# Differential attention on one core: the two maps of a head combined while they are turned, with one value product per head

## The chip, the cores and the metric

The kernel runs on one core of a Trainium2 chip. It is written by hand, engine by engine: TensorE (PE in the profile) multiplies, VectorE (DVE) and ScalarE (ACT) do the elementwise work, GpSimd (POOL) does next to nothing, SyncE (SP) issues the weight loads. The engines run side by side and wait for each other through semaphores. The metric is the device time of one execution in microseconds; several executions are taken, and their median counts.

## What is computed

The program is a whole forward pass: two layers of one model (attention, RWKV, two feed-forward stages) and two layers of a second one behind it. The change touches one stage, the differential attention of the second model, for 256 tokens, 8 heads, and two maps of width 64 in each head:

```python
q = q.reshape(bsz, seq, h, 2, d)          # h = 8 heads, 2 maps, d = 64
k = k.reshape(bsz, seq, h, 2, d)
v = v.reshape(bsz, seq, h, 2 * d)
lam_full = jnp.exp(jnp.sum(lamf[0] * lamf[1])) - jnp.exp(jnp.sum(lamf[2] * lamf[3])) + lambda_init
...
s = jnp.einsum('bqhcd,bkhcd->bhcqk', q_blk, k).astype(jnp.float32)
p = jax.nn.softmax(jnp.where(allowed, s, -jnp.inf), axis=-1)
p_diff = p[:, :, 0] - lam_full * p[:, :, 1]
return jnp.einsum('bhqk,bkhe->bqhe', p_diff.astype(v.dtype), v)
```

A query of chunk c (64 tokens) may look at the keys of chunks 0 to c. The output of each head is then normalised by its root mean square and goes through an output projection.

## The kernel before

All operands are f32. Tokens lie on the 128 partitions in two row tiles t = 0, 1. By the mask, row tile 0 needs 128 keys and row tile 1 needs 256, so a map has three 128 x 128 tiles (t, kt) = (0,0), (1,0), (1,1), and 384 score columns.

`attention()` (L948) is shared by all attentions of the program. The differential one calls it from `differential()` (L2087) with 16 maps, `diff=True` and `halves=True`. The work of a map m is a pipeline over the engines:

- TensorE, scores (L986): queries times keys, into a PSUM bank. With `halves`, the two maps of a head are issued together, on the two halves of the array's rows (64 each).
- VectorE, maxima (L1023): one pass that adds the mask, scales, writes the scores to SBUF and takes the row maximum, for each row tile.
- ScalarE, exps (L1072): exp with the maximum as bias, and the row sums, for each row tile.
- TensorE, turns (L997): three transposes of the exps, into another PSUM bank.
- ScalarE, copy (L1063): the turned tiles to SBUF.
- TensorE, products (L1005): turned tiles times values, three matmuls.
- VectorE, outputs: reciprocal of the row sums (L1035); for the second map of a head also the product with minus lambda (L1037, `nlam`); then the product of each row tile is scaled and written (L1046, first map), or scaled and added to the first map's output (L1044, second map). Row statistics of the finished head follow (L967).

The order on each engine is written out by a loop over i. Turns lag the scores by `TURN` = 2 maps and products by `MIX` = 3 maps. In iteration i TensorE issues the scores of maps i and i+1 (for even i), the turns of map i-2 and the products of map i-3. VectorE does the maxima of map i, then the outputs of map i-3; ScalarE copies the turned map i-2, then does the exps of map i. There are four buffers for exps, two banks for turned tiles, two for products, four for scores.

Behind the loop TensorE runs ten filler matmuls (L149) while VectorE forms the scales of all heads from the row statistics (L2110 to L2119) and ScalarE takes a root (L2102). The output projection begins with transposes of the scaled outputs (L437). The first norms of the program (L378) multiply by a diagonal of row scales instead of a plain identity; the 16 matmuls of one such norm are a like form to what the change adds.

## Time and profile before

| | us |
|---|---|
| median of 3 runs | 1690.74 |
| lowest and highest | 1688.20 and 1690.88 |
| the profiled execution | 1687.52 |
| span of its trace | 1685.70 |
| TensorE busy, whole span | 1647.3 (98%) |
| VectorE busy | 896.1 (53%) |
| ScalarE busy | 697.8 (41%) |
| GpSimd busy | 5.0 |
| first scores to last row statistics of this attention | 887.29 to 915.86 |

Times inside the trace count from the start of its span. A row of the timeline gives the start, the duration and the operation; rows that follow each other on an engine are merged ("x6"), and a note in brackets says how long the engine was idle before and what released it. Matmuls overlap: the start of the next one, not the duration of a row, tells what one costs. A plain f32 matmul leaves two rows, since it is made of two passes; a transpose leaves one. PEld is the loading of weights, which runs beside PE.

### The profile page before, as it was taken

How to read it: one execution, taken by the hardware profiler on the slowest of the kernel's cores; microseconds unless marked ns; L12 is line 12 of the kernel's file. 1: busy time of each engine (PE TensorE's matmuls, PEld its weight loads, DVE VectorE, ACT ScalarE, POOL GpSimd, SP SyncE). 2: the span in 40 equal slices, each digit the busy share in tenths (PEclk: the TensorE clock that was granted, in tenths of full speed). 3: DMA queues.
4: the chain of work that ended last, by engine and by line, in shares of the span. 5: the costliest groups of instructions: out<-in, count | busy, mean ns of one | idle time of the engine just before them, and what ended most of it. 6: DMA issues, size and time to landing. Idle time of an engine off the chain costs nothing.

```text
span 1685.7 us, 30187 instructions
## 1 busy us (share of the span) xinstructions
PE 1647.3 (98%) x12844; PEld 1288.1 (76%) x12844; DVE 896.1 (53%) x1932; ACT 697.8 (41%) x1347; POOL 5.0 (0%) x6
## 2 busy tenths in 40 slices
PE   9999999999999999999999999999989999999996
PEld 8889999787698699999887987555546798655553
DVE  6676565644567465658659765212126876521213
ACT  5576444433343354446548553111123655311111
POOL 0000000000000000000000000000000000000000
PEclk9999999999999999999999999999999999999998
DMA  8613453424200554535551446999992344699995
GB/s 343 250 76 151 160 216 131 165 100 150 89 3 13 228 186 160 216 107 194 199 186 40 176 167 261 425 424 426 423 421 76 113 186 172 261 426 424 425 425 226
DMA packets 36154, 371.69 MB, mean 220 GB/s; under 512 B 7200, under 2 KB 8352, under 8 KB 11184
## 3 DMA queue, kind: packets, MB, share of 16 engines
q1 hardware_dynamic: 32928, 364.09, 54.4%
q10 hardware_dynamic: 3088, 5.61, 1.0%
q8 instruction: 105, 1.72, 0.4%
q14 instruction: 33, 0.27, 0.0%
HBM read 368.63 MB, written 1.05 MB: 219 GB/s over the span
## 4 chain that ended last, share of the span: by engine, by line
PE 91%; DVE 5%; ACT 2%; DMA 1%; issue 1%; DVEq 0%; ACTq 0%
PE ps L660 41%; PE ps L2369 13%; PE ps L2392 6%; PE ps L884 3%; PE ps L2381 2%; PE ps L1005 2%; PE ps L1541 2%; PE ps L2352 2%; PE ps L1785 2%; PE ps L1754 2%; PE ps L986 1%; DMA ring<-in_w_moe 1%; PE ps L437 1%; PE ps L2856 1%; PE ps L2423 1%; PE ps L1768 1%
## 5 line engine op out<-in xcount | busy, mean ns | idle before, releaser
L660 PE MATMUL ps<-ffn_x_h,ffn_w 128*128 128x256 f32 x1408 | 257.4, 283 | 0.2
L2369 PE MATMUL ps<-ring,expert_inputs 128*64 128x256 f32 x1984 | 227.8, 382 | 0.7 <-DMA ring<-in_w_moe 0.7
L660 PEld LDWEIGHTS ps<-ffn_x_h,ffn_w 128*128 128x128 f32 x1408 | 221.2, 192 | 1.5 <-DVE ffn_x_l L499 0.5
L652 ACT CAST w_h<-ring 128x512 fp32r<-128x512 f32 x240 | 149.3, 624 | 138.1 <-PE ps L660 130.1
L660 PE MATMUL ps<-ffn_x_l,ffn_w 128*128 128x256 f32 x704 | 199.2, 283 | 0.0
L655 DVE TENSOR_TENSOR w_l<-ring,w_h 128x512 fp32r<-128x512 f32 x240 | 164.0, 689 | 66.0 <-ACT w_h L652 62.0
L2369 PEld LDWEIGHTS ps<-ring,expert_inputs 128*64 128x64 f32 x1984 | 137.0, 137 | 67.8 <-DMA ring<-in_w_moe 1.0
L655 DVE TENSOR_TENSOR ffn_w<-ring,ffn_w 128x1024 fp32r<-128x1024 f32 x132 | 155.8, 1220 | 20.9 <-ACT ffn_w L652 20.9
L660 PE MATMUL ps<-w_h,x_h 128*128 128x512 f32 x384 | 150.1, 391 | 0.0
L660 PE MATMUL ps<-w_h,x_l 128*128 128x512 f32 x384 | 149.5, 389 | 0.0
L660 PE MATMUL ps<-w_l,x_h 128*128 128x512 f32 x384 | 149.4, 389 | 0.0
L652 ACT CAST ffn_w<-ring 128x1024 fp32r<-128x1024 f32 x132 | 131.6, 1045 | 23.0 <-PE ps L660 23.0
L2504 ACT ACTIVATE routing<-ps 64x256 f32<-64x256 f32 x64 | 24.1, 377 | 272.3 <-PE ps L2369 272.3
L660 PEld LDWEIGHTS ps<-ffn_x_l,ffn_w 128*128 128x128 f32 x704 | 135.0, 192 | 0.7
L2631 DVE TENSOR_TENSOR routing<-routing,ps 64x256 f32<-64x256 f32 x64 | 27.2, 424 | 193.4 <-ACT routing L2504 193.4
L2392 PE MATMUL ps<-ring,routing 128*64 128x512 f32 x512 | 122.3, 598 | 0.8 <-DVE routing L2639 0.8
L660 PE MATMUL ps<-ffn_w,ffn_hid_h 128*128 128x512 f32 x352 | 108.8, 390 | 0.0
L1339 DVE SCALAR_TENSOR_TENSOR arena<-ps,cols,arena 128x255 f32<-128x255 f32 (+1 forms) x88 | 38.4, 478 | 89.8 <-ACT arena L1301 89.0
L660 PEld LDWEIGHTS ps<-w_h,x_l 128*128 128x128 f32 x384 | 72.1, 188 | 15.1
L660 PEld LDWEIGHTS ps<-w_h,x_h 128*128 128x128 f32 x384 | 72.1, 188 | 14.7
L660 PEld LDWEIGHTS ps<-w_l,x_h 128*128 128x128 f32 x384 | 72.1, 188 | 14.6
L2639 DVE COPY routing<-ps 128x128 f32<-128x128 f32 x64 | 18.5, 289 | 120.4 <-PE ps L2423 120.4
(377 smaller groups left out, 2657.4 us busy)
## 6 DMA issues: line engine op xcount, KB each, us to landing
ring<-in_w_moe SPq DMA_DIRECT2D x62, 2048.0 KB, 14.2
ring<-in_w_proj SPq DMA_DIRECT2D x37, 2048.0 KB, 7.8
ring<-in_w_ffn SPq DMA_DIRECT2D x22, 3072.0 KB, 10.2
ring<-in_w_moe SPq DMA_DIRECT2D x64, 1024.0 KB, 14.7
ring<-in_w_b_in SPq DMA_DIRECT2D x1, 2496.0 KB, 12.6
ring<-in_w_lora SPq DMA_DIRECT2D x1, 2048.0 KB, 7.6
rows<-in_w_moe SPq DMA_DIRECT2D x2, 1024.0 KB, 10.0
h<-in_w_moe SPq DMA_DIRECT2D x2, 1024.0 KB, 4.8
```

The source lines that it names most:

```text
L652: act.copy(high, x).then_inc(ready.up(), 1)
L655: return dve.tensor_tensor(low, x, high.bitcast(F32), ALU.subtract)
L660: last = pe.matmul(out, a[x], b[y], start=start and n == 0, stop=stop and n == 2, skip_group_check=True)
L884: last = pe.matmul(bank((n + 3 + m // 2) % 4)[:, (m % 2) * SEQ:(m % 2 + 1) * SEQ], w[:, k, m * P:(m + 1) * P], src[:, k, :], start=(k == 0 ...
L1005: last = pe.matmul(bank(o_bank[m % 2])[:, t * dv:(t + 1) * dv], pT[:, m % 2, c, :], v(m, kt), start=(kt == 0), stop=(kt == width[t] // P - 1))
L1339: ins = dve.scalar_tensor_tensor(x, gt[:, f, 0:SEQ - lag], col("conv_w", (layer * 3 + w) * FT + ft), x, ALU.mult, ALU.add)
L1541: last = pe.matmul(bank((n + 3 + t) % 4), mixes[x][:, k, t * P:(t + 1) * P], unit(i)[:, k, :], start=(k == 0), stop=(k == KD - 1))
L1754: last = pe.matmul(nt_out(q)[half(g), m % GROUP, w, :], x[1 - w], x[w], start=True, stop=True)
L1785: return pe.matmul(bank(OUT_BANK + 2 * t + u), xT[:, k, t * P:(t + 1) * P], w[:, k, :], start=(k == 0), stop=(k == KD - 1))
L2352: last = pe.matmul(o, parts_h[x][:, t, k * P:(k + 1) * P], put[:, t * D + q * QUAD:t * D + (q + 1) * QUAD], start=(t == 0 and x == 0), sto ...
L2369: last = pe.matmul(bank(0)[g * SLOTS_E:(g + 1) * SLOTS_E, 0:2 * P], x[:, k, e * SLOTS_E:(e + 1) * SLOTS_E], wg[g][:, k, :], start=(k == 0) ...
L2392: last = pe.matmul(bank(2)[c * SLOTS_E:(c + 1) * SLOTS_E, :], hids[:, f, :], wd[:, f, c * 512:(c + 1) * 512], start=(n % 2 == 0 and f == 0 ...
```

## The change

The differential attention gets a function of its own, `paired_attention()`, and its special cases leave `attention()`. It works in heads instead of maps.

The output of a head is r0 (P0 V) - lambda r1 (P1 V), where P0 and P1 are the exps of its maps, and r0, r1 the reciprocals of their row sums s0, s1. It is now formed as r0 ((P0 + c P1) V) with c = -lambda r1 s0, one number per query:

- VectorE forms the reciprocals of both maps at once (four numbers a row) and c (two numbers a row: the ratio).
- GpSimd multiplies the identity by c, for both row tiles, into a 128 x 256 buffer: two diagonal matrices.
- TensorE turns and combines at once: for each of the three tiles a plain matmul of the first map's exps with the identity, and one of the second map's exps with the diagonal, added in the same PSUM bank. (Before: one transpose for each tile of each map.)
- ScalarE copies once per head, and there is one set of products and one scaling per head, by r0.

The lags stay `TURN` = 2 and `MIX` = 3, but now count heads. Exps have room for three heads. The order per iteration i on VectorE is maxima of head i, ratio of head i-1, statistics of head i-4, outputs of head i-3; on ScalarE: exps of the first map, copy of head i-2, exps of the second map. GpSimd waits for the ratio and, from the third head on, for TensorE to have used the diagonal of two heads before.

The core of the diff (the new function, without its buffer declarations):

```diff
+        def paired_attention(q, k, v, o, scale, work):
...
+            DEPTH, TURN, MIX = 3, 2, 3
...
+            s_bank, p_bank, o_bank = ((6, 7), (0, 1)), (2, 3), (4, 5)
...
+                @block.tensor
+                def _(pe):
+                    for i in range(DIFF_HEADS + MIX):
...
+                        if i < DIFF_HEADS:
+                            if i >= 2:
+                                pe.wait_ge(s_out.sem, s_out.at(2 * T * (i - 1)))
+                            for t in range(T):
+                                for m in range(2):
+                                    last = pe.matmul(bank(s_bank[i % 2][m])[:, at[t]:at[t] + widths[t]], q(2 * i + m, t), k(2 * i + m)[:, 0:widths[t]], start=True, stop=True)
+                            last.then_inc(s_mm.up(), 1)
+                        if TURN <= i < DIFF_HEADS + TURN:
+                            hd = i - TURN
...
+                            if hd >= 2:
+                                pe.wait_ge(pT_ready.sem, pT_ready.at(hd - 1))
+                            pe.wait_ge(p_ready.sem, p_ready.at(2 * T * (hd + 1)))
+                            pe.wait_ge(diag_ready.sem, diag_ready.at(hd + 1))
+                            for c, (t, kt) in enumerate(tiles):
+                                pe.matmul(bank(p_bank[hd % 2])[:, c * P:(c + 1) * P], scores(hd, 0)[:, c * P:(c + 1) * P], ident[:], start=True, stop=False)
+                                last = pe.matmul(bank(p_bank[hd % 2])[:, c * P:(c + 1) * P], scores(hd, 1)[:, c * P:(c + 1) * P], diag[:, hd % 2, t, :], start=False, stop=True)
+                            last.then_inc(p_mm.up(), 1)
+                        if i >= MIX:
+                            hd = i - MIX
+                            pe.wait_ge(pT_ready.sem, pT_ready.at(hd + 1))
+                            if hd >= 2:
+                                pe.wait_ge(o_out.sem, o_out.at(hd - 1))
+                            for c, (t, kt) in enumerate(tiles):
+                                last = pe.matmul(bank(o_bank[hd % 2])[:, t * P:(t + 1) * P], pT[:, hd % 2, c, :], v(hd, kt), start=(kt == 0), stop=(kt == t))
+                            last.then_inc(o_mm.up(), 1)
+
+                @block.gpsimd
+                def _(pool):
+                    for hd in range(DIFF_HEADS):
+                        pool.wait_ge(ratio_ready.sem, ratio_ready.at(hd + 1))
+                        if hd >= 2:
+                            pool.wait_ge(p_mm.sem, p_mm.at(hd - 1))
+                        one = ident[:].rearrange("p (o s) -> p o s", o=1).broadcast_to([P, T, P])
+                        c = ratio[:, hd % 2, :].rearrange("p (t o) -> p t o", o=1).broadcast_to([P, T, P])
+                        pool.tensor_tensor(diag[:, hd % 2], one, c, ALU.mult).then_inc(diag_ready.up(), 1)
...
+                    def ratios(hd):
+                        b = hd % DEPTH
+                        dve.wait_ge(p_ready.sem, p_ready.at(2 * T * (hd + 1)))
+                        if hd >= DEPTH:
+                            dve.wait_ge(o_out.sem, o_out.at(hd - DEPTH + 1))
+                        link(dve, "dve_step", dve.reciprocal(rs[:, b], sums[:, b]))
+                        if hd >= 2:
+                            dve.wait_ge(diag_ready.sem, diag_ready.at(hd - 1))
+                        dve.scalar_tensor_tensor(ratio[:, hd % 2, :], rs[:, b, 1, :], nlam[:], sums[:, b, 0, :], ALU.mult, ALU.mult).then_inc(ratio_ready.up(), 1)
...
+                    for i in range(DIFF_HEADS + MIX):
+                        if i < DIFF_HEADS:
+                            maxima(i)
+                        if 1 <= i <= DIFF_HEADS:
+                            ratios(i - 1)
+                        if i > MIX:
+                            statistics(i - MIX - 1)
+                        if i >= MIX:
+                            outputs(i - MIX)
+                    statistics(DIFF_HEADS - 1)
...
+                    for i in range(DIFF_HEADS + TURN):
+                        if i < DIFF_HEADS:
+                            exps(i, 0)
+                        if i >= TURN:
+                            turned(i - TURN)
+                        if i < DIFF_HEADS:
+                            exps(i, 1)
```

How the order changes is seen at one head in the middle. TensorE before, from one set of scores on (`arena2_12` holds queries, keys, exps and turned tiles, `arena1_9` the values and outputs, `ident` the identity; `probs_ready` counts exps, `act_evacuated` copies of turned tiles):

```order
L986 MATMUL ps<-arena2_12 128x128 [waits scores_copied]
L986 MATMUL ps<-arena2_12 128x128
L986 MATMUL ps<-arena2_12 128x256 x2
L997 MATMUL ps<-ident,arena2_12 128x128 [waits act_evacuated,probs_ready]
L997 MATMUL ps<-ident,arena2_12 128x128 x2
L1005 MATMUL ps<-arena1_9,arena2_12 128x128 [waits dve_evacuated,act_evacuated]
L1005 MATMUL ps<-arena1_9,arena2_12 128x128 x2
L997 MATMUL ps<-ident,arena2_12 128x128 [waits act_evacuated,probs_ready]
L997 MATMUL ps<-ident,arena2_12 128x128 x2
L1005 MATMUL ps<-arena1_9,arena2_12 128x128 [waits dve_evacuated,act_evacuated]
L1005 MATMUL ps<-arena1_9,arena2_12 128x128 x2
```

and after, from one set of scores on (`conv_ready` is the semaphore of GpSimd's diagonals):

```order
L981 MATMUL ps<-arena2_12 128x128 [waits scores_copied]
L981 MATMUL ps<-arena2_12 128x128
L981 MATMUL ps<-arena2_12 128x256 x2
L992 MATMUL ps<-ident,arena2_12 128x128 [waits conv_ready,probs_ready,act_evacuated]
L993 MATMUL ps<-arena2_12 128x128
L992 MATMUL ps<-ident,arena2_12 128x128
L993 MATMUL ps<-arena2_12 128x128
L992 MATMUL ps<-ident,arena2_12 128x128
L993 MATMUL ps<-arena2_12 128x128
L1001 MATMUL ps<-arena1_9,arena2_12 128x128 [waits act_evacuated]
L1001 MATMUL ps<-arena1_9,arena2_12 128x128 x2
```

Two groups of three transposes and two groups of three products, each group with its waits, have become one group of six matmuls, which also waits for the diagonal, and one of three.

VectorE before, from the outputs of a first map to those of the second (`ISA` rows are the maxima and the reading of their result):

```order
L1035 RECIPROCAL stat<-stat 128x2 [waits probs_ready]
L1046 TENSOR_SCALAR arena1_9<-ps,stat 128x128 [waits product_ready,dve_step]
L1046 TENSOR_SCALAR arena1_9<-ps,stat 128x128
L967 BN_STATS arena0_0<-arena1_9 128x6 [waits dve_evacuated]
L1023 ISA arena2_12,stat<-ps,mask 128x128 [waits transposed,scores_ready]
L1023 ISA stat 128x1
L1023 ISA arena2_12,stat<-ps,mask 128x256
L1023 ISA stat 128x1
L1035 RECIPROCAL stat<-stat 128x2 [waits probs_ready]
L1037 TENSOR_SCALAR stat<-stat,nlam 128x2 [waits dve_step]
L1044 SCALAR_TENSOR_TENSOR arena1_9<-ps,stat,arena1_9 128x128 [waits dve_evacuated,product_ready,dve_step]
L1044 SCALAR_TENSOR_TENSOR arena1_9<-ps,stat,arena1_9 128x128
```

and after, from the maxima of a head's second map into the next head:

```order
L1026 ISA arena2_12,stat<-ps,mask 128x128
L1026 ISA stat 128x1
L1026 ISA arena2_12,stat<-ps,mask 128x256
L1026 ISA stat 128x1
L1034 RECIPROCAL stat<-stat 128x4 [waits dve_evacuated,probs_ready]
L1037 SCALAR_TENSOR_TENSOR stat<-stat,nlam 128x2 [waits conv_ready,dve_step]
L1048 BN_STATS arena0_0<-arena1_9 128x6 [waits dve_evacuated]
L1048 BN_STATS arena0_0<-arena1_9 128x6
L1042 TENSOR_SCALAR arena1_9<-ps,stat 128x128 [waits product_ready]
L1042 TENSOR_SCALAR arena1_9<-ps,stat 128x128
L1026 ISA arena2_12,stat<-ps,mask 128x128 [waits transposed,scores_ready]
L1026 ISA stat 128x1
```

The two outputs of the second map are gone, the reciprocals are one instruction of four numbers, the ratio takes the place of the product with lambda, and it stands right behind the maxima, before the outputs. Nothing else in the program moves on TensorE, VectorE or ScalarE; GpSimd's eight instructions stand ahead of the two it had.

## Rows read from the trace of the kernel before

**Rows 1.** Busy time: start:end, length, busy us (count) of PE, PEld, DVE, ACT, POOL, clock.

```profile
887.29:914.24 26.95, 24.97 (x210) 20.88 (x210) 24.02 (x131) 24.06 (x83) 0.00 (x0) 1.00 0.01 2
```

**Rows 2.** TensorE in order of time, one head: start us, us, engine, line, operation.

```profile
904.00 0.93 PE L986 MATMUL ps<-arena 64*128 64x128 f32 x8
904.86 0.55 PE L997 MATMUL ps<-ident,arena 128*128 128x128 f32 x3
905.24 0.83 PE L1005 MATMUL ps<-arena,arena 128*128 128x128 f32 x6
905.91 0.49 PE L997 MATMUL ps<-ident,arena 128*128 128x128 f32 x3
...
907.00 0.93 PE L986 MATMUL ps<-arena 64*128 64x128 f32 x8
```

**Rows 3.** VectorE in order of time, the same head.

```profile
904.28 0.27 DVE L1023 CUSTOM_DVE_ANT_0 arena<-ps,mask 128x128 f32<-128x128 f32 x1
...
904.83 0.16 DVE L1035 RECIPROCAL stat<-stat 128x2 f32<-128x2 f32 x1
...
906.29 0.16 DVE L1035 RECIPROCAL stat<-stat 128x2 f32<-128x2 f32 x1
906.49 0.23 DVE L1037 TENSOR_SCALAR stat<-stat,nlam 128x2 f32<-128x2 f32 x1
906.75 0.61 DVE L1044 SCALAR_TENSOR_TENSOR arena<-ps,stat,arena 128x128 f32<-128x128 f32 x2
907.28 0.28 DVE L967 BATCH_NORM_STATS2 arena<-arena 128x6 f32<-128x128 f32 x1
907.48 0.27 DVE L1023 CUSTOM_DVE_ANT_0 arena<-ps,mask 128x128 f32<-128x128 f32 x1
```

**Rows 4.** ScalarE in order of time, the same head.

```profile
904.66 0.40 ACT L1072 ACTIVATE arena<-arena,stat 128x128 f32<-128x128 f32 x1 [0.37 <-DVE stat L1023]
...
905.55 0.46 ACT L1063 COPY arena<-ps 128x384 f32<-128x384 f32 x1
906.12 0.40 ACT L1072 ACTIVATE arena<-arena,stat 128x128 f32<-128x128 f32 x1
```

**Rows 5.** One pass of 16 matmuls on a diagonal, and one of 16 transposes.

```profile
7.84 3.88 PE L378 MATMUL ps<-arena,h 128*128 128x128 f32 x32
...
L437 PE MATMUL ps<-ident,h x16: 272/273/328, 946.1 to 948.1; 128*128 128x128 f32 x16
```

**Rows 6.** All that GpSimd ran, by group: count | busy us, mean ns | idle before.

```profile
L2655 POOL TENSOR_TENSOR token_l<-h,token_h 128x1024 fp32r<-128x1024 f32 x2 | 4.8, 2400 | 1435.7 <-ACT token_h L2456 1435.7
L3084 POOL MEMSET const-float32-0.0<- 128x1 f32 x1 | 0.1, 98 | 0.2 <-issue 0.2
```

**Rows 7.** All engines in order of time, the start of this attention.

```profile
887.29 1.58 PE L986 MATMUL ps<-arena 64*128 64x128 f32 x16
...
888.39 0.29 DVE L1023 CUSTOM_DVE_ANT_0 arena<-ps,mask 128x128 f32<-128x128 f32 x1 [0.30 <-PE ps L986]
...
889.99 0.52 PE L997 MATMUL ps<-ident,arena 128*128 128x128 f32 x3 [1.12 <-ACT arena L1072]
...
890.53 0.19 ACT L1072 ACTIVATION_READ_ACCUMULATOR arena<-arena,stat 128x1 f32 x1
```

**Rows 8.** All engines in order of time, its end.

```profile
912.47 1.77 PE L1005 MATMUL ps<-arena,arena 128*128 128x128 f32 x12
...
914.08 4.48 PE L149 MATMUL ps<-ident 128*128 128x256 f32 x20
...
915.19 0.67 DVE L967 BATCH_NORM_STATS2 arena<-arena 128x6 f32<-128x128 f32 x3
...
918.48 0.66 PE L437 MATMUL ps<-ident,arena 128*128 128x128 f32 x4
```

**Rows 9.** Stretches near the end of the program, columns as in the first.

```profile
1672.00:1674.00 2.00, 0.33 (x4) 0.26 (x4) 0.75 (x1) 0.69 (x1) 0.00 (x0) 1.00 0.00 0
...
1676.00:1678.00 2.00, 0.00 (x0) 0.00 (x0) 1.66 (x6) 1.98 (x3) 0.00 (x0) 0.75 0.00 0
```

More of the change, by code:

```diff
@@ L43 @@
 HEADS, HD = 16, 64
+DIFF_HEADS = 8
 ALPHA = 4.0 ** 0.25
@@ L954, in attention @@
+        def attention(maps, q, k, v, dv, o, scale, masked, work, halves=False):
             TURN, MIX = 2, 3
@@ L963, in attention @@
             ns, group = len(s_bank), 2 if halves else 1
-            def head_stats(dve, o_out, head, t):
-                dve.wait_ge(o_out.sem, o_out.at(2 * head + 2))
-                dve.bn_stats(head_bn[:, 8 * t + head, :], o(2 * head, t)).then_inc(sig("row_stats").up(), 1)
             with new_block() as block:
@@ L1035, in _ @@
                             link(dve, "dve_step", dve.reciprocal(rs[:, b, :], sums[:, b, :]))
-                            if diff and m % 2:
-                                link(dve, "dve_step", dve.tensor_scalar(rs[:, b, :], rs[:, b, :], nlam[:], None, ALU.mult))
                             dve.wait_ge(o_mm.sem, o_mm.at(m + 1))
-                            if diff and m % 2:
-                                dve.wait_ge(o_out.sem, o_out.at(m))
                             for t in range(T):
                                 x, r = bank(o_bank[m % 2])[:, t * dv:(t + 1) * dv], rs[:, b, t:t + 1]
-                                if diff and m % 2:
-                                    ins = dve.scalar_tensor_tensor(o(m, t), x, r, o(m, t), ALU.mult, ALU.add)
-                                else:
-                                    ins = dve.tensor_scalar(o(m, t), x, r, None, ALU.mult)
+                                ins = dve.tensor_scalar(o(m, t), x, r, None, ALU.mult)
                             ins.then_inc(o_out.up(), 1)
-                            if diff and m >= 2:
-                                head_stats(dve, o_out, m // 2 - 1, m % 2)
-                    if diff:
-                        for t in range(T):
-                            head_stats(dve, o_out, maps // 2 - 1, t)
                 @block.scalar
@@ L2086, in differential @@
             o = tok(5)
-            attention(16, lambda m, t: [fm(6)[hs(m), m // 2, t * P:(t + 1) * P]], lambda m: [fm(7)[hs(m), m // 2, :]],
-                      lambda m, kt: tok(4)[:, kt, (m // 2) * P:(m // 2 + 1) * P], P, lambda m, t: o[:, t, (m // 2) * P:(m // 2 + 1) * P],
-                      HD ** -0.5, True, (blk(8), blk(9)), diff=True, halves=True)
+            paired_attention(lambda m, t: fm(6)[hs(m), m // 2, t * P:(t + 1) * P], lambda m: fm(7)[hs(m), m // 2, :],
+                             lambda hd, kt: tok(4)[:, kt, hd * P:(hd + 1) * P], lambda hd, t: o[:, t, hd * P:(hd + 1) * P], HD ** -0.5, (blk(8), blk(9)))
             with new_block() as block:
```

57 lines of the change are left out of this document (56 added, 1 removed).

## The prediction

> **What bounds the kernel now.** I read the span and TensorE's share first, then the stage that the diff touches, then one head of it on each engine. TensorE is the busiest engine of the whole program, so the question is how long it takes through the differential attention. In this stretch, 26.95 us long, it is busy 24.97 us, VectorE 24.02 and ScalarE 24.06 [rows 1]: three engines run nearly level, so neither of them alone is "the" bound, and the period of each has to be taken apart.
>
> TensorE: one head goes scores, turns, products, turns, products, scores again. The starts lie 0.86, 0.38, 0.67, then 1.09 us apart, together 3.00 us from one set of scores to the next [rows 2]. Six passes of products take 0.67 us, 0.111 us a pass. The scores cost 0.86 whatever follows them.
>
> VectorE: the same head takes 907.48 - 904.28 = 3.20 us without an idle note [rows 3]. So VectorE falls 0.2 us behind TensorE per head, and the reader sees it in ScalarE, which waits 0.37 us for the maxima at 904.66 [rows 4]. ScalarE's own work is shorter: 905.55 - 904.66 = 0.89 us for two exps with their sums and 0.46 at most for the copy, twice, so 2.7 us per head at most. The stage is thus bound by TensorE at 3.00 at first, by VectorE at 3.20 towards its end, plus a start and an end at which one engine waits for another [rows 7, 8]. The end of the stage is the last of the row statistics at 915.19 + 0.67 = 915.86; behind it VectorE forms the head scales, and only then TensorE goes on at 918.48, its filler matmuls (from 914.08, 4.48 us) being about over by then [rows 8].
>
> **TensorE's work, part by part.** A transpose is one pass per tile (three rows for three tiles), a plain f32 matmul two (six rows for three tiles) [rows 2]. The new turn of a head is two plain matmuls on each of three tiles, the first with the identity, the second with the diagonal: 3 x 2 x 2 = 12 passes, where the two maps had 2 x 3 = 6. That a product with a diagonal is also two passes is seen elsewhere in this kernel: 16 such matmuls leave 32 rows in 3.88 us, against 16 rows for 16 transposes [rows 5]. The value products fall from 12 passes to 6. So +6 and -6 passes: 26 per head before and after, counting the 8 of the scores. With the same spacing the head is 0.86 (scores) + 0.05 + 12 x 0.111 = 1.38 (turns) + 0.76 (six passes and the change back to scores, which is 1.09 - 0.33) = **3.00 us**. The change buys nothing on TensorE. Bounds: 0.119 us a pass, from the 32 rows of [rows 5] (3.88 less the last pass's 0.2, over 31), would make it 3.10; 0.10 with fewer switches between kinds would make it 2.9.
>
> **VectorE.** Per head it loses one reciprocal (0.20), the product with lambda (0.26) and the second pair of outputs (0.53), and gains one two-element operation for the ratio, as long as the lambda product it replaces (0.26 at most, 0.20 by the reciprocal) [rows 3]. Left are 3.20 - 0.99 + 0.20 = 2.4 us, so VectorE drops under TensorE's 3.00. **ScalarE** loses one of two copies, 0.46 us per head [rows 4], and is at 2.2. Both have cover now; what is next late is TensorE itself. Over the heads that VectorE bound before (those after about 904, where ScalarE shows its waits) this frees some 0.2 us each, about 1 us in all.
>
> **GpSimd.** It has no work here before. It gets one 128 x 256 product per head. Its only like row is 128 x 1024 at 2.40 us, and an instruction of one element takes 0.10 [rows 6]. In proportion that is 0.10 + 2.30 / 4 = **0.68 us**. Both ends are 0.10 and 2.40; I take 0.68, since the row it comes from is the same operation on the same type of data. In steady state it hides: the scores of head h+1 begin, 1.10 later VectorE starts the maxima [rows 7], four of them take 2 x 0.55 = 1.10 [rows 3], the ratio of head h 0.40, GpSimd 0.68, with some 0.1 at each change of engine 3.4 to 3.5; TensorE wants that diagonal after 3.00 (next scores) + 0.86 = 3.86. The slack is 0.4 us. Behind the waiting turn on TensorE stand the products of the head before and the scores of the head after next, so what is late there is late for all.
>
> **The lag at both ends.** The pipeline's distance is now counted in heads. Before, the first turn comes at 889.99, after the exps of one map [rows 7]. Now it needs the exps of both maps: the fourth exp's sum is read at 890.53 + 0.19 = 890.72 in the trace, and this order stays. Then the ratio (0.40, to 891.2), GpSimd (0.1 + 0.68) and the hop: **first turn at 892.1**, 2.1 us later than before. From there, by the lengths above: scores of head 3 at 893.45, turn 1 at 894.3, product 0 at 895.7, scores of heads 4, 5, 6 and 7 at 896.45, 899.45, 902.45 and 905.45. Before, the scores of heads 6 and 7 stand at 904.00 and 907.00 in the same series [rows 2], so in this measure the new order is 1.5 us ahead, since it issues three heads of scores before the first turn. At the end this is paid back, since two turns and three products are still left where before there were two maps and a half: turn 5 at 906.3, product 4 at 907.7; the diagonal of head 6 is ready at 905.45 + 1.10 + 1.10 + 0.40 + 0.85 = 908.9, half a microsecond after TensorE would like it; turn 6 908.9, product 5 910.25, turn 7 910.9, product 6 912.25; the copy of turn 7 (0.46, and two hops) lets product 7 begin at 913.0 and end at 913.85; outputs 0.61 and two statistics 0.5 bring the **end to about 915.3**. Before it was 915.86: a gain of 0.5 us. The same placing with the old order gives 915.8, so it holds to some 0.1 where all lengths are measured. The filler matmuls and the scales move with it.
>
> **The sum.** -0.5 us on the profiled execution, whose 1687.52 (span 1685.70) becomes 1687.0. The median of the runs shown is 3.2 above it, at 1690.74, so the forecast there is **1690.2**. A bound on the terms: GpSimd at 0.10 would take the first turn to 891.5 and end the stage at 914.7 or so (-1.2); 3.10 per head instead of 3.00 adds 0.8; GpSimd at 1.0 adds 0.6.
>
> **Rivals.**
> (1) *GpSimd is slow and becomes the bound* (the slower side). The ring is scores h+1, maxima, ratio, diagonal, turn h, product h-1, scores h+3: 1.10 + 1.10 + 0.40 + 0.2 + d + 1.38 + 0.76 = 4.9 + d for two heads, against 6.0. It decides from d = 1.1 us. Below that, d counts only at the first and the last turns, twice; above it, about four times. At d = 2.0: 2 x 0.4 + 4 x 0.9 - 0.5 = +3.9 us, 1694.6; at the bound of 2.40, +5.5, 1696.2. Against it stands the proportion above [rows 6]; for it that GpSimd's fixed cost on two broadcast operands is not in the trace. 7 in 100 for more than 3.4 us.
> (2) *VectorE and GpSimd block each other.* If VectorE stands still while GpSimd works, its 2.4 us become 3.1 to 3.2, as before, and the gain of the late heads is lost: +1.1, 1691.8. No row of before has both at work on this. 12 in 100. The Trainium skill, "SBUF — State Buffer", section "Who interferes with whom", says that the two share a port pair that one of them locks for a whole instruction, but only against VectorE instructions with two SBUF inputs or in a 2-port mode. The long ones here (maxima, outputs) read one operand from PSUM, so by that rule the block would be short and this rival falls; nothing in the trace of before can show it.
> (3) *A diagonal product costs one pass, like a transpose.* Then TensorE would need 2.4 us per head and VectorE would bound at 2.4 to 2.5: -4, 1686.6. [rows 5] speak against it. 3 in 100.
> (4) *The clock falls in the gap before the first turn*, which grows from 1.1 idle us [rows 7] to some 1.5, on either side of the third scores. TensorE's granted clock stayed at 1.00 (2.4 GHz) over 1672 to 1674, in which it was busy 0.33 of 2 us, and fell only later, in a stretch without any matmul (0.75 on average) [rows 9]. If it fell to 1.2 GHz for only one head's work, +3; 2 in 100.
>
> **How the numbers follow.** Forecast 76, rivals 7, 12, 3 and 2. A measurement of this kernel can tell about 0.2%, 3.4 us, from no change. The forecast and rival 2 lie inside; rivals 1 and 4 give slower, rival 3 faster, with two or three in 100 added to each side since the runs shown, with the profiled one, spread from 1687.5 to 1690.9 by themselves. So same 0.86, faster 0.05, slower 0.09. The range takes this spread below the forecast and, above it, rival 2 and a part of rival 1: 1687.2 to 1692.8.
>
> **What would show it.** Right: scores of the heads 3.0 us apart on TensorE with 12 rows of turns; the first turn near 892 in the old time scale; a GpSimd row near 0.7 us; VectorE idle some 0.5 us per head; the last statistics end 28.0 us after the first scores (28.6 before). Wrong: a GpSimd row over 1.1 us with TensorE idle before each turn (rival 1); maxima or outputs longer than before or begun only when GpSimd ends (rival 2); 6 rows of turns per head (rival 3); a granted clock under 1.00 (rival 4).

## The result and the profile after

The changed kernel takes 1695.47 us in the median of 6 runs (1694.03 to 1699.1); the kernel before, beside it, 1689.11 (6 runs, 1686.81 to 1690.88). The ratio is 1.004, 95% interval 1.003 to 1.005: **slower by 6.4 us**, 0.4%, which is small but clear of the noise, where no change was forecast. The profiled execution took 1694.46 with a span of 1692.7, 7.0 more than before.

First the attention. TensorE in the changed kernel, one head in order of time (start, us, engine, line, operation), answers to [rows 2]:

```profile
904.69 0.93 PE L981 MATMUL ps<-arena 64*128 64x128 f32 x8
905.55 0.49 PE L992 MATMUL ps<-ident,arena 128*128 128x128 f32 x2
905.88 0.39 PE L993 MATMUL ps<-arena 128*128 128x128 f32 x2
...
906.99 0.83 PE L1001 MATMUL ps<-arena,arena 128*128 128x128 f32 x6
907.75 0.93 PE L981 MATMUL ps<-arena 64*128 64x128 f32 x8
```

From scores to scores 3.06 us, where 3.00 stood before. VectorE in the same head, and GpSimd's groups, answer to [rows 3, 6]:

```profile
904.80 0.61 DVE L1042 TENSOR_SCALAR arena<-ps,stat 128x128 f32<-128x128 f32 x2 [0.25 <-PE ps L1001]
905.67 0.29 DVE L1026 CUSTOM_DVE_ANT_0 arena<-ps,mask 128x128 f32<-128x128 f32 x1 [0.25 <-PE ps L981]
...
906.99 0.22 DVE L1037 SCALAR_TENSOR_TENSOR stat<-stat,nlam 128x2 f32<-128x2 f32 x1
907.13 0.48 DVE L1048 BATCH_NORM_STATS2 arena<-arena 128x6 f32<-128x128 f32 x2
907.86 0.61 DVE L1042 TENSOR_SCALAR arena<-ps,stat 128x128 f32<-128x128 f32 x2 [0.26 <-PE ps L1001]
```

```profile
L1012 POOL TENSOR_TENSOR arena<-ident,stat 128x256 f32<-128x256 f32 x8 | 4.9, 614 | 907.4 <-DVE stat L1037 907.4
L2776 POOL TENSOR_TENSOR token_l<-h,token_h 128x1024 fp32r<-128x1024 f32 x2 | 4.8, 2388 | 531.1 <-ACT token_h L2577 531.1
```

VectorE now waits for TensorE twice a head, 0.25 and 0.26 us, where it had no idle note before; a diagonal costs GpSimd 0.61 us. But for the 0.06 us per head, this is as forecast. The start of the stage is not. TensorE there, which answers to [rows 7]:

```profile
892.44 0.46 PE L992 MATMUL ps<-ident,arena 128*128 128x128 f32 x2 [1.44 <-ACT arena L1069]
...
893.62 0.63 PE L992 MATMUL ps<-ident,arena 128*128 128x128 f32 x2
894.04 0.64 PE L993 MATMUL ps<-arena 128*128 128x128 f32 x2
894.61 1.65 PE L981 MATMUL ps<-arena 64*128 64x128 f32 x8
```

The first turn comes when it should, but from 893.2 on the same instructions take longer, a set of scores 1.65 us instead of 0.93. The busy time by stretches says why (start:end, length, busy us of PE, PEld, DVE, ACT, POOL, granted clock):

```profile
893.20:896.60 3.40, 3.40 (x18) 2.52 (x17) 0.45 (x4) 1.92 (x8) 0.61 (x1) 0.50 0.02 5
896.60:908.00 11.40, 11.40 (x100) 9.92 (x101) 8.90 (x52) 8.83 (x35) 2.46 (x4) 1.00 0.00 1
```

For 3.4 us the granted clock is 0.50, 1.2 GHz, with TensorE busy all the time; it fell 0.8 us after TensorE had resumed from the 1.44 idle us. Ahead of that lie another 0.79 idle us, on the other side of the scores of head 2, which start at 890.08. The stage, from the first scores to the end of the last statistics, takes 29.86 us (887.71 to 917.57) against 28.57 (887.29 to 915.86).

That is 1.3 of 7.0 us. The rest lies 340 us later, where the diff changes nothing. The first expert stage ends there, and the 16 transposes that turn the normalised rows follow. TensorE in the kernel before:

```profile
1254.28 1.19 PE L2381 MATMUL ps<-expert_rows 64*128 64x512 f32 x8 [1.67 <-DVE expert_rows L2627]
1260.53 3.64 PE L437 MATMUL ps<-ident,h 128*128 128x128 f32 x16 [5.06 <-DVE h L403]
1263.99 10.40 PE L2856 MATMUL ps<-ring,xT 128*128 128x312 f32 x39
```

and in the changed one:

```profile
1255.80 1.19 PE L2502 MATMUL ps<-expert_rows 64*128 64x512 f32 x8 [1.67 <-DVE expert_rows L2748]
1262.35 0.69 PE L438 MATMUL ps<-ident,h 128*128 128x128 f32 x2 [5.36 <-DVE h L404]
1268.34 3.25 PE L438 MATMUL ps<-ident,h 128*128 128x128 f32 x14 [5.30 <-issue]
1271.38 2.87 PE L2977 MATMUL ps<-ring,xT 128*128 128x312 f32 x9
```

Two transposes, then 5.30 us in which TensorE waits for nothing that the profile shows, then the other fourteen. From the last products to the next stage's first (L2381 to L2856, now L2502 to L2977) 9.71 us became 15.58. The account of the 7.0 us: +0.42 ahead of the attention, +1.29 up to the matmuls behind it (L660 at 920.96, now L661 at 922.67), -0.19 up to the end of the experts, **+5.87 here**, -0.4 behind.

**What the stop is.** The two branches of the expert stage stand one behind the other in the program, the sparse one first; it is executed and ends with a jump over the dense one, to the code of these transposes. Of the fetching of instructions the trace shows one thing, the packets of an instruction queue (q8), 16384 bytes each. In the kernel before, one such packet starts at 1258.0 and is there at 1259.09, and TensorE starts the transposes at 1260.53, 1.44 us later; the next packet starts at 1264.0. In the changed kernel they start at 1259.8 and 1265.8. The first is there at 1260.91, and the transposes start at 1262.35, 1.44 us later; the second is there at 1266.87, and TensorE goes on at 1268.34, 1.47 us later. Two stretches of the changed kernel's DMA view, 1259.7 to 1261 and 1265.7 to 1267, each hold one:

```profile
q8 instruction: 1, 0.02, 5.3%
```

```profile
q8 instruction: 1, 0.02, 5.2%
```

The same distance stands in all twelve traces of this case: the transposes behind the jump start 1.42 to 1.45 us after the first packet has landed, whatever the attention before them was like. So it is the packet that sets their start, in the kernel before too, and not VectorE, to which the profile puts the idle time down (5.06 us <-DVE h L403). The first of the three VectorE instructions of that line, the one that the first transpose waits for in the code, is through at 1259.82 in the kernel before and at 1261.34 in the changed one, 0.7 and 1.0 us ahead of TensorE's start.

The Trainium skill ("Runtime: NRT & Kernel Launch", section "Instruction fetch mechanics") says that instructions come in blocks of 16 KiB, 256 instructions, one fetched ahead while another runs, and that a taken branch breaks this order. The packets' size agrees. The section gives no price, and calls the crossing of a block's border mostly hidden; the 5.30 us put down to "issue" here speak against that for the first border behind a jump.

So the theory is: *only the block of the jump's target is fetched by the jump, the one behind it some 6 us later. Where the target stands near the end of its block, TensorE runs dry.* The changed attention has 14 TensorE instructions fewer, all of them waits. That count is the author's and stands in no view of the profile; that e2 below, shifted by 242 = 256 - 14, stops after the same two transposes bears it out. With one offset, fitted to the stop in the changed kernel, the target moves from place 10 of its block, 246 instructions left, to place 252, 4 left. Two transposes are 4 instructions, a weight load and a matmul each. The offset is fitted, so these two places alone prove nothing; the runs with other shifts do.

### The profile page after: what moved, and what is told of

Same layout as the page of the kernel before. It is cut to its first block, busy times and chain, and to the rows that moved or that the text cites. A ratio compares the mean times of both kernels' runs of the same rounds, so it can differ in the third digit from the quotient of the medians.

```text
span 1692.7 us, 30128 instructions
## 1 busy us (share of the span) xinstructions
PE 1649.3 (97%) x12844; PEld 1289.7 (76%) x12844; DVE 890.9 (53%) x1908; ACT 695.2 (41%) x1339; POOL 9.9 (1%) x14
## 4 chain that ended last, share of the span: by engine, by line
PE 93%; DVE 4%; ACT 2%; issue 1%; DVEq 0%; ACTq 0%
PE ps L661 41%; PE ps L2490 13%; PE ps L2513 7%; PE ps L885 3%; PE ps L2502 2%; PE ps L1663 2%; PE ps L1139 2%; PE ps L2473 2%; PE ps L1907 2%; PE ps L1876 2%; PE ps L1120 1%; PE ps L438 1%; PE ps L2544 1%; PE ps L2977 1%; PE ps L1890 1%
## 5 line engine op out<-in xcount | busy, mean ns | idle before, releaser
L661 PE MATMUL ps<-ffn_x_h,ffn_w 128*128 128x256 f32 x1408 | 257.4, 283 | 0.2
L661 PEld LDWEIGHTS ps<-ffn_x_h,ffn_w 128*128 128x128 f32 x1408 | 221.2, 192 | 1.5 <-DVE ffn_x_l L500 0.5
L661 PE MATMUL ps<-ffn_x_l,ffn_w 128*128 128x256 f32 x704 | 199.2, 283 | 0.0
L661 PE MATMUL ps<-w_h,x_h 128*128 128x512 f32 x384 | 150.1, 391 | 0.0
L661 PE MATMUL ps<-w_h,x_l 128*128 128x512 f32 x384 | 149.5, 389 | 0.0
L661 PE MATMUL ps<-w_l,x_h 128*128 128x512 f32 x384 | 149.4, 389 | 0.0
L661 PEld LDWEIGHTS ps<-ffn_x_l,ffn_w 128*128 128x128 f32 x704 | 135.0, 192 | 0.7
L661 PE MATMUL ps<-ffn_w,ffn_hid_h 128*128 128x512 f32 x352 | 108.9, 390 | 0.0
L661 PEld LDWEIGHTS ps<-w_h,x_l 128*128 128x128 f32 x384 | 72.1, 188 | 15.0
L661 PEld LDWEIGHTS ps<-w_l,x_h 128*128 128x128 f32 x384 | 72.1, 188 | 14.8
L661 PEld LDWEIGHTS ps<-w_h,x_h 128*128 128x128 f32 x384 | 72.1, 188 | 14.7
```

The source lines that it names most:

```text
L661: last = pe.matmul(out, a[x], b[y], start=start and n == 0, stop=stop and n == 2, skip_group_check=True)
```

## The experiments

Rivals to this theory were that something in the new attention leaves TensorE or a queue in another state (then the place of the code would not matter), that the weight transfers or the time at which the stage ends bring it about, and that the slower attention is the whole loss and the stop is covered elsewhere. The kernel before ran beside all of them, at 1689.2 to 1689.3 us in the median. "Dead" transposes stand in the dense branch of the first expert stage, which is never executed: they change only where the code behind them stands.

**The changed kernel again.**

> The changed kernel once more, beside the three below on the same chip. Before, it took 6.4 us more than the kernel before (1695.47 to 1689.11). The two traces put that into two places: about 1.3 us in the changed attention, where the granted clock reads 0.50 for 3.4 us from the first turn on, and about 5.9 us behind the first expert stage, where TensorE stops for 5.30 us after two transposes with no wait that the trace shows. Expected: +6 us again, in all theories.

1696.33 us (6 runs), ratio 1.0043, 1.0028 to 1.0059. The stop is there, 5.40 us. But in its profiled execution the granted clock stays at 1.00 in the attention. The stretch that answers to the slow one above:

```profile
893.20:896.60 3.40, 3.40 (x31) 2.95 (x30) 1.70 (x11) 2.96 (x14) 0.64 (x2) 1.00 0.02 5
```

31 rows of matmuls where 18 stood. The stage takes 28.29 us (887.74 to 916.03). So the same code has the fall of the clock in some executions and not in others, and between these two it is worth 1.57 us. GpSimd works beside the first turns in both (from 893.43 and from 893.47), so it is not what makes the rows slow.

**The target moved away from the block's end.** 14 dead instructions give back what the change took:

```diff
+                        for n in range(7 if layer == 0 else 0):
+                            pe.transpose(bank(0)[:, 0:P], ident[:], ident[:])
                         for n in range(2 * T):
                             pe.transpose(bank(0)[:, 0:P], ident[:], ident[:]).then_inc(summed.up(), 1)
```

> The changed kernel with seven transposes more (14 TensorE instructions) in the dense branch of the first expert stage, which is jumped over in every run: nothing more is executed. The changed attention has 14 instructions fewer on TensorE than before (all of them waits), so the code behind it stands 14 places earlier. Theory code place: the stop of 5.3 us comes from where the target of the jump over the dense branch stands in the blocks in which instructions are fetched; 14 places later it is gone, so 5.3 us less than the changed kernel, +1 us to the kernel before; the transposes behind the jump run on without a gap. Rival load: the stop comes from the weight transfers or from the time at which the stage ends; then nothing changes and it stays at +6 us.

1689.79 us (12 runs), ratio 1.0007, 0.9996 to 1.0018: the loss of the medians is gone, 6.5 us less than the changed kernel beside it. TensorE:

```profile
1262.04 3.48 PE L438 MATMUL ps<-ident,h 128*128 128x128 f32 x16 [4.98 <-DVE h L404]
```

The attention in this profile is the slow one (29.86 us, clock 0.50 from 893.1 to 896.6), so the time came back by the place of the code alone. The experts end at the same time as in the changed kernel (last products from 1255.86, there 1255.80), and the stop is gone: the time of the stage's end does not bring it about, nor do the weight transfers by themselves, which are the same.

**The kernel before, with its target moved to the same place.** The same edit with 121 dead transposes, 242 instructions; its attention is untouched.

> The kernel before, without the change, with 121 transposes more (242 TensorE instructions) in the same branch that is never executed. 242 is 14 short of 256, the number of instructions in one fetched block of 16384 bytes at 64 bytes each, so the target of the jump stands in its block where it stands in the changed kernel. Theory code place: the kernel before gets the stop of 5.3 us although its attention is the old one, so about +5.3 us. Rival load or time: no difference, 0.

1695.65 us (6 runs), ratio 1.0042, 1.0025 to 1.0058. The old attention takes its old 28.56 us, and the stop appears:

```profile
1263.07 0.69 PE L437 MATMUL ps<-ident,h 128*128 128x128 f32 x2 [5.36 <-DVE h L403]
1268.96 3.25 PE L437 MATMUL ps<-ident,h 128*128 128x128 f32 x14 [5.21 <-issue]
```

The stop comes after two transposes, as in the changed kernel. With this pair the rivals fall: the new attention without the stop costs nothing that the medians show, and the stop without the new attention costs all of it.

**How much must be left in the block.** The edit of e1 in the changed kernel with 120 and with 100 dead transposes, which leaves 20 and 60 instructions.

> The changed kernel with 120 transposes (240 TensorE instructions) in the branch that is jumped over, so that 20 instructions of a block are left behind the target of the jump instead of 4 (in e1 246). Theory code place: TensorE gets through 10 of the 16 transposes there before it stops, and goes on when the next block has come, at the same time after the jump as in the changed kernel; the stop is then some 3.5 us instead of 5.3, the whole about 1.5 to 2 us less than the changed kernel and 4 to 5 us more than e1. Rival: a stop is all or nothing for any place near the end of a block; then it is as in the changed kernel.

1695.62 us (7 runs), ratio 1.0047, 1.0031 to 1.0064.

```profile
1260.64 2.40 PE L438 MATMUL ps<-ident,h 128*128 128x128 f32 x10 [5.14 <-DVE h L404]
1266.47 1.54 PE L438 MATMUL ps<-ident,h 128*128 128x128 f32 x6 [3.43 <-issue]
```

The stop comes after exactly 10 transposes, 20 instructions, and is as short as forecast. The total is not: where 1.5 to 2 us less than the changed kernel were expected, it is as slow. The products behind tell why. First and last start of the 64 matmuls there in e6, then in the changed kernel (ns min/median/max, starts):

```profile
L2979 PE MATMUL ps<-ring,xT x64: 426/426/728, 1267.8 to 1286.6; 128*128 128x312 f32 x64
```

```profile
L2977 PE MATMUL ps<-ring,xT x64: 426/426/727, 1271.4 to 1288.3; 128*128 128x312 f32 x64
```

In e6 they take 18.8 us from start to start, in the changed kernel 16.9. The granted clock is at 0.50 until 1272.4 in the one and 1272.1 in the other, so e6 begins its products 4.6 us before the clock is back, and runs them at half speed: ten in this stretch of e6 (columns as above), one every 0.52 us, where one every 0.26 us runs behind it.

```profile
1267.80:1272.40 4.60, 4.60 (x10) 3.04 (x10) 4.12 (x5) 0.42 (x1) 0.00 (x0) 0.51 0.01 4
```

What the shorter stop saved was lost to this: from the experts' last products (1254.31, there 1255.80) to the last start here, e6 takes 32.3 us, the changed kernel 32.5.

> The same with 100 transposes: 60 instructions are left behind the target. Theory code place: the 16 transposes (32 instructions) and 14 matmuls more run before the block ends, by then the next one has come: no stop or one under 0.5 us, so the time of e1, 5 to 6 us less than the changed kernel. Rival: the number of dead instructions itself (a longer jump) costs, then it is as slow as e6.

1690.43 us (12 runs), ratio 1.0003, 0.9993 to 1.0014; no stop (16 transposes in one row, 3.67 us). One of the twelve executions took 6264.64 us; it stands outside the ratio, nothing on record explains it, and the median of the other eleven is 1689.69. 60 instructions are enough here, and the longer jump itself costs nothing. The attention of its profile had the low clock (stage 29.87).

**The idle time before the first turn filled.** In the changed kernel, one filler matmul behind the scores of head 1 and three behind those of head 2:

```diff
+                        if i in (1, 2):
+                            for x in end["first_turns"] if i == 1 else ():
+                                pe.wait_ge(*x)
+                            fill(pe, {1: 1, 2: 3}[i], 2)
                         if TURN <= i < DIFF_HEADS + TURN:
```

> The changed kernel with four filler matmuls of the identity (16 TensorE instructions) in the two stretches in which TensorE waits before the first turn: one behind the scores of head 1, three behind those of head 2, into a bank that the first turn overwrites. They also move the code behind by +16, past the place of the stop. Theory clock: the granted clock stays at 1.00 through this attention, which takes 28.1 us from the first scores to the last statistics instead of 29.9, so 1.7 us less than the kernel with the shift alone, and -0.5 to -1 us against the kernel before. Rival: the slow rows (0.21 instead of 0.11 us a pass) at the first turn come from GpSimd reading the same memory beside; then they stay slow with the fillers, and the time is that of the shift alone.

1689.66 us (12 runs), ratio 0.9996, 0.9985 to 1.0007. No stop, since the fillers move the target as well (place 13). TensorE has only 0.16 us of idle time left at the start:

```profile
890.11 0.93 PE L981 MATMUL ps<-arena 64*128 64x128 f32 x8 [0.16 <-DVE stat L1030]
890.96 1.56 PE L150 MATMUL ps<-ident 128*128 128x256 f32 x6
892.48 0.46 PE L996 MATMUL ps<-ident,arena 128*128 128x128 f32 x2
...
893.98 0.93 PE L981 MATMUL ps<-arena 64*128 64x128 f32 x8
```

The first turn is not later for them, the stage takes 28.30 us, where 28.1 were expected, and the rows of the first turns are not slow, though GpSimd works beside them. In the profiles of the changed attention without fillers the clock fell in three of five (the changed kernel, e1, e7; not e0, e6); with them in none of five (e3, e4, e5, and the two below). If the fillers did nothing, three falls in ten profiles would all lie on one given side by chance in one case of twelve: that the idle time brings the clock down is likely, not shown. The medians of e1 and e3 differ by 0.13 us, where 1.7 were expected, so that the gain is not resolved in time.

**GpSimd's share three times as long.** e3 with each diagonal formed three times over (those who wait for a diagonal wait for the third, which is not shown):

```diff
+                        for _ in range(2):
+                            link(pool, 'conv_ready', pool.tensor_tensor(diag[:, hd % 2], one, c, ALU.mult))
                         pool.tensor_tensor(diag[:, hd % 2], one, c, ALU.mult).then_inc(diag_ready.up(), 1)
```

> The kernel with fillers (e3), with each diagonal formed three times in a row by GpSimd, one after the other, and released after the third: 3 x 0.61 us and two handovers, some 1.95 us instead of 0.61. Theory ring: the diagonal hides for the heads in the middle as long as it takes under some 1.2 us; the loop from the scores of head h+1 over maxima, ratio, diagonal, turn and product to the scores of head h+3 then takes 4.9 + 1.95 = 6.85 us for two heads instead of 6.1, so 0.35 us more per head, and at the first and the two last turns the added 1.34 us shows as a whole: together +4 to +5 us against e3. Rival hidden: GpSimd is beside the path altogether, 0. Rival port: GpSimd's reading holds up VectorE's maxima or outputs; then their rows (0.28, 0.42, 0.35 us) are longer than in e3.

1693.89 us (10 runs), ratio 1.0027, 1.0017 to 1.0037; the stage takes 32.73 us, 4.43 more than in e3. TensorE waits for GpSimd at every second head:

```profile
899.66 0.93 PE L981 MATMUL ps<-arena 64*128 64x128 f32 x8
901.34 0.46 PE L996 MATMUL ps<-ident,arena 128*128 128x128 f32 x2 [0.75 <-POOL arena L1018]
...
903.51 0.93 PE L981 MATMUL ps<-arena 64*128 64x128 f32 x8
904.39 0.46 PE L996 MATMUL ps<-ident,arena 128*128 128x128 f32 x2
...
906.57 0.93 PE L981 MATMUL ps<-arena 64*128 64x128 f32 x8
908.25 0.46 PE L996 MATMUL ps<-ident,arena 128*128 128x128 f32 x2 [0.75 <-POOL arena L1018]
```

Two heads take 6.91 us (899.66 to 906.57), with 2.0 us from GpSimd's first start to its last end (902.25 to 904.25). The ring of rival 1, 4.9 + d, gives 6.9. It is there, and at 0.61 us it has room.

This run also tests rival 2, since GpSimd works here into the maxima of a head. GpSimd, then VectorE in e4:

```profile
899.20 1.30 POOL L1017 TENSOR_TENSOR arena<-ident,stat 128x256 f32<-128x256 f32 x2 [2.16 <-DVE stat L1043]
900.58 0.61 POOL L1018 TENSOR_TENSOR arena<-ident,stat 128x256 f32<-128x256 f32 x1
```

```profile
900.63 0.29 DVE L1032 CUSTOM_DVE_ANT_0 arena<-ps,mask 128x128 f32<-128x128 f32 x1 [0.26 <-PE ps L981]
...
900.85 0.42 DVE L1032 CUSTOM_DVE_ANT_0 arena<-ps,mask 128x256 f32<-128x256 f32 x1
```

The two maxima begin while GpSimd is at work and take 0.29 and 0.42 us, as in e3, where it is not; the outputs from 903.62, with GpSimd at work until 904.25, take their 0.61.

**The diagonals on VectorE.** e3 without GpSimd: two multiplications of the identity by one column per head, with the waits that follow from it (not shown).

```diff
+                        for t in range(T):
+                            ins = dve.tensor_scalar(diag[:, hd % 2, t, :], ident[:], ratio[:, hd % 2, t:t + 1], None, ALU.mult)
+                        ins.then_inc(diag_ready.up(), 1)
```

> The kernel with fillers (e3), with the two diagonal tiles of a head formed by VectorE (two tensor_scalar of 128 x 128 right behind the ratio) instead of GpSimd. VectorE has some 0.5 us per head free in the trace of the changed kernel, and these take about 0.2 to 0.3 us each if they run like the one-input pass of 128 columns (0.28 us), so the period stays at TensorE's 3.06 and the first turn comes as early or up to 0.3 us earlier than with GpSimd: between -0.5 and +0.5 us against e3. Rival: VectorE is full and becomes the bound: 3.2 us per head, +1.

1688.28 us (12 runs), ratio 0.9994, 0.9986 to 1.0003; stage 27.95 us. The two take VectorE 0.48 us, in idle time that it has, and save a change of engine before the first and the last turns: 0.35 us of the stage, 0.12 of it at the first turn and the rest at the seventh. The medians of e5 and e3 lie 1.4 us apart, more than was expected and more than the stage accounts for; the rest is not explained. The other VectorE work runs beside no GpSimd here: row statistics 0.48, outputs 0.59, against 0.48 and 0.61 above.

**An attempt to beat both.** In e5 the clock is low for 10 us around the end of the experts, where TensorE idles 5.00 us. Fillers at the end of the executed branch, ahead of its jump, 6 or 10 of them:

```diff
                         scatter(N_EXPERTS - 1, summed)
+                        fill(pe, 10 if layer == 0 else 0, 0)
                     either(pe, dense, sparse)
```

> The kernel of e5 (diagonals by VectorE, four filler matmuls at the start of the attention) with 6 filler matmuls more at the end of TensorE's sparse branch of the first expert stage, ahead of its jump; the jump's target moves from slot 13 to slot 37. In e5 TensorE has no matmul from 1255.1 to 1260.1 there, its granted clock is 0.50 from then to about 1265, and the 16 transposes of L438 take 3.67 us. If this idle time is what brings the clock down, six fillers (4.48 us / 20 = 0.22 us a row, 2 rows each, 2.7 us in all, to about 1257.8) shorten the idle time to 2.3 us: transposes nearer to the 2.0 us of a full clock, 1 to 2 us less than e5, 1687. If the jump is taken only when the fillers are through, and needs a fetch and 1.47 us, TensorE would resume at 1259.3 at the earliest and nothing would be lost, since it waits for VectorE until 1260.1.

> As e8 with 10 fillers, 4.5 us, to about 1259.6; target slot 53. If only idle time matters: the transposes of L438 at the full clock, 1.5 to 2.5 us less than e5, 1686. If the jump waits for the fillers' end and costs a fetch of 1.0 and 1.47 us behind it: TensorE resumes at 1261 to 1262 instead of 1260.1, which takes back 1 to 2 us, and e9 is no better than e8, about 1687 to 1688.

1688.98 us, ratio 0.9992, 0.9982 to 1.0002, and 1688.85 us, ratio 0.9998, 0.9989 to 1.0008 (12 runs each): no gain over e5, where 1 to 2 us were expected of e8. TensorE in e8, then in e9:

```profile
1256.71 2.86 PE L150 MATMUL ps<-ident 128*128 128x256 f32 x12
1262.20 3.05 PE L438 MATMUL ps<-ident,h 128*128 128x128 f32 x16 [2.63 <-DVE h L404]
```

```profile
1255.16 4.58 PE L150 MATMUL ps<-ident 128*128 128x256 f32 x20
1262.28 3.51 PE L438 MATMUL ps<-ident,h 128*128 128x128 f32 x16 [2.54 <-issue]
```

The low stretch shrinks from 10 us to 3.4, but begins about when the transposes do, which still take 3.05 and 3.51 us. The packet for the jump starts when the fillers end, at 1259.67 in e8 and 1259.74 in e9, and TensorE goes on 1.4 us after it has landed, as everywhere. In e8, measured from the experts' last products, this is 0.4 us later than in e5, and the 16 transposes give back 0.6. In e9 it is 2.1 us later, and 2.7 us after VectorE's result was there. A version clearly faster than the kernel before was not found; e5 is 1.0 us below it, inside its interval.

## Why the prediction was wrong, point by point

- **"Nothing else in the program moves"** (the part on the change) is the step that failed, and the sum rests on it: its one term, -0.5 us, is that of the attention, and the 770 us behind it are put at nothing without a reason. Nothing moves in order, but the code moves in place. 14 instructions fewer put a jump's target 4 instructions before the end of a block: 5.30 us of stop, and 5.87 us in all between the same two products. Shown by e1 and e2, from both sides. None of the four rivals holds it.
- **Rival 4, the clock**, had its chance and size wrong, and its cause probably right. It was given 2 in 100 and +3 us, on the strength of [rows 9], where the clock stayed at 1.00 over two microseconds with TensorE busy 0.33 of them. It fell here in three of five profiled executions, and cost 1.57 us. Some 1.5 idle us were forecast on either side of the third scores; 0.79 ahead of them and 1.44 behind came. What [rows 9] show is one case in which the clock held, not that it holds.
- **TensorE's 3.00 us per head** measured 3.06. The passes are 26 as said, and the spacing of the turns 1.44 instead of 1.38 us (905.55 to 906.99). Over five heads this is 0.3 us: the stage at full clock is 28.29 us, where 28.0 were forecast and 28.57 stood before, a gain of 0.3 instead of 0.5.
- **The first turn** was forecast at 892.1 in the old scale, 4.8 us behind the first scores; it comes at 892.44, 4.7 behind them. The step-by-step placing from old rows held, and so did scores of head 3: 6.16 us behind the first ones forecast, 6.24 measured in e0.
- **GpSimd at 0.68 us** by proportion from [rows 6]: 0.61. **Rival 1** (bound from d = 1.1) did not come, and e4 shows that it was priced well: at d = 2.0 it gave +3.9 us, and the stage of e4 is 4.16 us above the kernel before.
- **Rival 2** did not come. Row statistics (907.13) run while GpSimd works (907.29 to 907.90) in 0.48 us, as in e5 without it, and the maxima and outputs of e4 take under GpSimd's work what they take without. The rule of the Trainium skill ("SBUF — State Buffer", section "Who interferes with whom"), by which VectorE instructions with one SBUF input, outside the 2-port modes, are not blocked: these rows agree.
- **Rival 3** did not come: 12 rows of turns.
- **VectorE** idles 0.5 us per head, as forecast. ScalarE's relief bought nothing by itself either.

The gain that the change was built for is 0.3 us in this chain, since VectorE's and ScalarE's savings lie beside a TensorE that does as many passes as before.

**What stays open.** What the 1.4 us between the packet's end and the next matmul are, and why the second packet starts some 6 us after the first, in the kernel before and in the changed one alike. One rival for the second was not tried: the weight transfers fill the DMA engines until shortly before it. Three stretches, of the kernel before, whose second packet starts at 1264.0, and of e9, where it starts at 1265.14 (columns as above; DMA share and GB/s last):

```profile
1259.20:1263.00 3.80, 2.48 (x12) 2.48 (x13) 2.00 (x6) 1.83 (x3) 0.00 (x0) 0.50 1.01 425
1263.20:1264.00 0.80, 0.80 (x6) 0.80 (x5) 0.33 (x1) 0.62 (x2) 0.00 (x0) 0.51 0.82 348
```

```profile
1262.50:1265.10 2.60, 2.60 (x13) 2.60 (x13) 0.81 (x2) 1.02 (x2) 0.00 (x0) 0.50 0.64 271
```

In eleven of the twelve traces the second packet starts 0.5 to 1.5 us after the share has begun to fall from full, in e9 2.1 us after. So the 6 us, and with them the length of the stop, may hang on this load; the place of the code decides only whether TensorE has to wait for the packet. A run with other transfers at this point would tell. Between 20 instructions left (a stop) and 60 (none) the border was not looked for. The executions of the kernel before alone lie between 1686.8 and 1695.1 us, so that differences of a microsecond rest on the traces, one a kernel. What decides in which executions the clock falls in the attention was not found.

## What to carry to other kernels

A kernel with branches or loops has places where TensorE starts in fresh code behind a jump; there, the number of instructions ahead of the place, executed or not, waits too, is worth microseconds, and any edit can shift it. When a measured change doesn't lie where the diff is, compare the traces stage by stage, look for an idle time put down to "issue" behind a jump, and move the code by a few dead instructions before judging the edit itself. An idle time behind a jump that the profile puts down to another engine can be the fetch all the same: compare its end with the instruction packet's. And where an edit lets TensorE idle for over a microsecond before dense work, price a fall of the clock, here 1.6 us, since one row in which it held proves little.

## What the runs showed of the hardware

- Behind a taken jump TensorE had only the rest of the target's block: 4 instructions left, stops of 5.21 to 5.40 us; 20 left, 3.43 us; 60 and more, none. The transposes behind the jump started 1.42 to 1.45 us after the first 16384-byte packet had landed, in all twelve traces. The second packet began 5.4 to 6.1 us after the first, under DMA engines that were full for most of that time, and where TensorE had stopped it went on 1.36 to 1.47 us after that had landed.
- The stop also holds the clock down: the granted clock, at 0.50 from 1257.2 to 1264.0 before, stays there from 1258.4 to 1272.1. In e6, with a stop 1.9 us shorter, it stays until 1272.4, which is why that saved nothing.
- After idle times of 0.79 and 1.44 us the clock fell to 1.2 GHz for 3.4 us, in some executions of the same code and not in others.
- A 128 x 256 product of two broadcast operands takes GpSimd 0.61 us, and VectorE 0.48 us as two products with a column.
